# Attention of the first block: the values of one unit ahead of the transposes of the next on TensorE

## The chip, the cores and the metric

The kernel runs on one core of a Trainium2 chip. The core has five engines with a queue of instructions each: TensorE (PE) for matrix products, VectorE (DVE), ScalarE (ACT), GpSimd (POOL) and SyncE (SP), which here issues the DMAs. Each takes its instructions strictly in the order of the program, and waits on semaphores for the others. The metric is the device time of one execution in microseconds.

## The reference

Two transformer blocks of depth 2 each run one after the other on 256 tokens of width 1024. In the first, each layer mixes three kinds of heads, and the attention kinds among them are these:

```python
        s_c = jnp.einsum('bqghd,bngd->bghqn', qb, kc)
        p_c = _masked_softmax(s_c, cmp_end[None, :] <= t[:, None])
        o_c = jnp.einsum('bghqn,bngd->bqghd', p_c, vc)
...
        o_s = jnp.einsum('bghqkl,bgqkld->bqghd', p_s, v_sel)
...
        o_w = jnp.einsum('bghqk,bkgd->bqghd', p_w, vwb)
...
        return gb[:, :, 0, :, :, None] * o_c + gb[:, :, 1, :, :, None] * o_s + gb[:, :, 2, :, :, None] * o_w
```

and, for the third kind of head,

```python
        s = jnp.einsum('bqhd,bkhd->bhqk', qb, kh) + cq[..., None] - c[:, :, None, :]
        p = _masked_softmax(s, kpos[None, :] <= t[:, None])
        return jnp.einsum('bhqk,bkhd->bqhd', p, vh)
```

The second block needs a modulation vector, silu(c) @ w_ada (1024 x 9216 a layer), that depends on nothing in the first.

## The kernel before

The first reference block runs as two layers, l = 0 and 1; below, "block 0" and "block 1" are these two passes through the same code, in which the attention stands once. Their attention lies at 174 to 268 us and 656 to 750 us of the span.

The attention is cut into 22 units (`units_block1`): for each half of the 128-row query tiles (tt = 0, then 1) a "cmp" unit for the compressed keys of all heads, then "slc" and "win" units in turn, four of each, for two heads each, then two "fox" units. In the first half a unit has 128 keys, in the second 256. A unit passes through these steps, each with a semaphore:

- TensorE, `unit_scores` (L986, L997, L1003; L994 and L1002 for fox): scores of the unit into a bank, att_s.
- VectorE, `unit_max`: row maximum (L1072, L1074), att_m.
- ScalarE, `unit_exp` (L1125): exponential and row sum, att_e.
- VectorE, `unit_norm` (L1095 to L1103): the rows scaled by gate over sum, att_p.
- TensorE, `unit_turn` (L1015; L1012 for cmp): the probabilities transposed into bank 6, two or four 128x128 transposes. It waits for att_p of this unit and att_c of the one before; att_t.
- ScalarE, `unit_copy` (L1137; L1132 for cmp): bank 6 to SBUF, att_c.
- TensorE, `unit_values` (L1034; a slc unit has first L1028, the compressed part): probabilities times values into bank 7. It waits for att_c of this unit, and at a unit that opens an output for the output before, att_o; att_v. A cmp unit has none.
- ScalarE, `unit_out` (L1144): bank 7 out, once a win or fox unit is done, att_o.

The loops are software-pipelined by turns n = 0 to 23. On TensorE a turn is: scores of unit n+1, a part of the modulation (`ada_pe`), transposes of unit n-1, values of unit n-2. On VectorE: maximum of unit n, `ada_dve`, norm of unit n-1. On ScalarE: exponential of unit n, copy of n-1, output of n-2, `ada_act`.

The modulation is filled in between: in every turn `ada_pe` takes two 512 KB chunks of w_ada from a ring of four slots (L856, 32-column tiles, 8 rows in the trace) and, in turns 0 and 1 and all odd turns after, folds a finished row first (L844). A fold waits for the ScalarE copy of the row in the turn before (`ada_act`, L866), and VectorE takes the fold's result (L872) in the same turn, ahead of its norm. A slot freed by L856 lets SyncE ask for the chunk four further on. Behind the attention comes the output product (L774 on), whose weights use the same ring.

The order is written out by hand; no scheduler moves it. The loop in question is `attention_pe`, from L1040.

Of the kernel before, what the change touches and what calls it, by code (L numbers as in the profile page):

```python
# [502 lines left out]
def kernel_program(nc, streams, consts, params, x_cm, ctx_cm, out_cm, blocks=(1, 2)):  # L503
    with ExitStack() as stack:
# [320 lines left out]
        def ada_bank(l, q):  # L825
            return bank[1 + 2 * ((ADA_QUADS * l + q) % 2)]

        def ada_chunk(l, i):
            a, own, b = PLAN["in_a", l].chunk, PLAN["ada", l].chunk, PLAN["wo", l].chunk
            chunk = a + 2 * i + 1 if i < 7 else own + i - 7 if i < 7 + ADA_ALONE else b + 2 * (i - 7 - ADA_ALONE) + 1  # L830
            return chunk % SLOTS, chunk // SLOTS

        def ada_started(t):
            return range(ADA_UPTO[t - 1] if t else 0, ADA_UPTO[t])

        def ada_done(t):

            return [q for q in range(ADA_QUADS) if t >= 0 and 4 * q + 3 in ada_started(t)]

        def ada_pe(pe, l, t):  # L840
            for q in ada_done(t - 2):
                pe.wait_ge(s.ada_row, ADA_QUADS * l + q + 1)
                for j in range(4):
                    mm = pe.matmul(ada_bank(l, q)[:, 2 * j:2 * j + 2], ada_row[:, j * P:(j + 1) * P], fold,  # L844
                                   start=True, stop=True)
                mm.then_inc(s.ada_t, 1)
            for m in ada_started(t):
                q, c = m // 4, m % 4
                slot, turn = ada_chunk(l, m)
                if c == 0 and ADA_QUADS * l + q >= 2:  # L850
                    pe.wait_ge(s.ada_out, ADA_QUADS * l + q - 1)
                pe.wait_ge(landed[slot], (turn + 1) * 16)
                for i in range(2):
                    k = 2 * c + i
                    rows = slice(k % COL_GROUPS * COL_GROUP, (k % COL_GROUPS + 1) * COL_GROUP)
                    mm = pe.matmul(ada_bank(l, q)[rows, :], cs[:, k, :], ring[:, slot, i * 4 * P:(i + 1) * 4 * P],  # L856
                                   start=(k < COL_GROUPS), stop=(k >= COL_GROUPS))
                mm.then_inc(used[slot], 1)
# [120 lines left out]
        def unit_scores(pe, x):  # L979
            if x.u >= 2:  # L980
                pe.wait_ge(s.att_e, x.u - 1)
            q = slice(x.tt * P, (x.tt + 1) * P)
            if x.kind == "cmp":
                for h in range(QH):
                    rows = slice(h % 2 * DH, h % 2 * DH + DH)
                    mm = pe.matmul(half_scores(x, h % 2)[:, h // 2 * N_CMP:(h // 2 + 1) * N_CMP], qr[rows, h // 2, q],  # L986
                                   kcb[rows, h // 4 * N_CMP:(h // 4 + 1) * N_CMP], start=True, stop=True)
                mm.then_inc(s.att_s, 1)
                return
            for hh in range(2):  # L990
                rows = slice(hh * DH, hh * DH + DH)
                dst = half_scores(x, hh)[:, 0:x.keys]
                if x.kind == "fox":
                    pe.matmul(dst, qkn[rows, 6 + x.j, q], qkn[rows, 8 + x.j, 0:x.keys], start=True, stop=False)  # L994
                else:
                    key = kd[rows, x.g, 0 if x.kind == "slc" else 1, 0:x.keys]
                    pe.matmul(dst, qr[rows, 2 * x.g + x.j, q], key, start=True, stop=False)  # L997
            for hh in range(2):
                dst = half_scores(x, hh)[:, 0:x.keys]
                if x.kind == "fox":  # L1000
                    for st in range(x.kt):
                        pe.matmul(dst, fa[:, st, 2 * x.j + hh, q], gtk[:, st, 0:x.keys], start=False, stop=False)  # L1002
                mm = pe.matmul(dst[:, x.keys - P:x.keys], ident, causal, start=False, stop=True)  # L1003
            mm.then_inc(s.att_s, 1)

        def unit_turn(pe, x):

            pe.wait_ge(s.att_p, x.u + 1)
            if x.u >= 1:
                pe.wait_ge(s.att_c, x.u)  # L1010
            if x.kind == "cmp":
                mm = pe.transpose(bank[6][0:heads_n, 0:P], pr[:, x.u % 2, 0:heads_n], ident)  # L1012
            else:
                for c in range(2 * x.kt):
                    mm = pe.transpose(bank[6][:, c * P:(c + 1) * P], pr[:, x.u % 2, c * P:(c + 1) * P], ident)  # L1015
            mm.then_inc(s.att_t, 1)
# [3 lines left out]
        def unit_values(pe, x):  # L1020
            if x.kind == "cmp":
                return
            pe.wait_ge(s.att_c, x.u + 1)
            if x.first and x.o >= 1:
                pe.wait_ge(s.att_o, x.o)
            if x.kind == "slc":
                h = 4 * x.g + 2 * x.j
                pe.matmul(bank[7][:, 0:P], own_b[0:heads_n, h * DH:(h + 2) * DH], c_pt[0:heads_n, x.tt, :],  # L1028
                          start=True, stop=False, skip_group_check=True)
            for k in range(x.kt):  # L1030
                for hh in range(2):
                    head = 2 * x.j + hh if x.kind == "fox" else x.g
                    c0 = VCOL[x.kind] + head * DH
                    mm = pe.matmul(bank[7][hh * DH:(hh + 1) * DH, 0:P], vtok[:, k, c0:c0 + DH],  # L1034
                                   pt[:, x.v % 2, (hh * x.kt + k) * P:(hh * x.kt + k + 1) * P],
                                   start=(x.kind == "fox" and k == 0), stop=(x.last and k == x.kt - 1),
                                   skip_group_check=True)
            mm.then_inc(s.att_v, 1)

        def attention_pe(pe, l, units):  # L1040
            unit_scores(pe, units[0])
            for n in range(len(units) + 2):
                if n + 1 < len(units):
                    unit_scores(pe, units[n + 1])
                ada_pe(pe, l, TICK_ATT + n)
                if 1 <= n <= len(units):
                    unit_turn(pe, units[n - 1])
                if n >= 2:
                    unit_values(pe, units[n - 2])

        def unit_max(dve, x):

# [353 lines left out]
        def block1_pe(pe, l):  # L1406
# [87 lines left out]
            pe.wait_ge(s.vc_done, l + 1)  # L1494
            pe.wait_ge(s.fa, l + 1)
            attention_pe(pe, l, units_block1(l))

            lin = PLAN["wo", l]
# [1094 lines left out]
```

## Time and profile before

| | us |
|---|---|
| three timed executions | 3120.65, 3120.95, 3123.78 |
| their median | 3120.95 |
| the profiled execution | 3125.64 |
| its span in the trace | 3123.9 |
| TensorE busy in it | 2961.4 (95%) |
| VectorE busy | 1519.0 (49%) |
| ScalarE busy | 1129.8 (36%) |

The profile is of one execution, not among the three. "Busy" of TensorE has modelled ends, so that durations of neighbours overlap in the timeline; the starts are what was recorded. An fp32 matmul shows as two records, one of fp32r and a transpose as one. A group in the timeline merges like instructions that follow each other, and a wait inside a group shows only as a longer group.

### The profile page before, as it was taken

What the parts mean: (1) busy time and instruction counts of PE and PEld (TensorE: products, weight loads), DVE (VectorE), ACT (ScalarE), POOL (GpSimd) and SP (SyncE); (2) the same over time, 40 slices, a digit from 0 to 9 for tenths busy, and PEclk for the clock granted to TensorE, in tenths of its full rate; (3) what the DMA queues carried; (4) which work ended last, traced back from release to release, by engine and by line L of the source; (5) the groups of instructions that cost most, each with busy time, mean ns of one, the idle gap of its engine ahead of it and who ended that gap; (6) DMA issues with size and microseconds to landing.
All of it is one profiled execution on the core that took longest, in us unless ns stands there. A gap on an engine that the chain in (4) does not pass through costs nothing.

```text
span 3123.9 us, 46087 instructions
## 1 busy us (share of the span) xinstructions
PE 2961.4 (95%) x17140; PEld 2426.9 (78%) x17140; DVE 1519.0 (49%) x2621; ACT 1129.8 (36%) x1727; POOL 45.3 (1%) x36
## 2 busy tenths in 40 slices
PE   6998998989999999999999999999999998999998
PEld 6756998846898888877466678888788887688998
DVE  5344655434656333349433464333433336645664
ACT  4333544333544222133355332222322223385443
POOL 0100000000000000002000000000000000000000
PEclk9999999999999999999999999999999998999999
DMA  4576454476554222321122122223222222234454
GB/s 172 186 264 223 164 179 155 155 275 232 185 175 141 95 94 92 100 84 58 61 74 65 63 85 96 99 92 96 88 94 101 91 99 93 74 116 137 164 181 137
DMA packets 119881, 400.91 MB, mean 128 GB/s; under 512 B 13008, under 2 KB 22608, under 8 KB 119504
## 3 DMA queue, kind: packets, MB, share of 16 engines
q1 hardware_dynamic: 116816, 393.27, 37.5%
q10 hardware_dynamic: 2944, 6.01, 0.5%
q8 instruction: 78, 1.28, 0.2%
q14 instruction: 43, 0.35, 0.0%
HBM read 398.18 MB, written 1.05 MB: 128 GB/s over the span
## 4 chain that ended last, share of the span: by engine, by line
PE 84%; DVE 8%; ACT 3%; DMA 2%; DVEq 2%; issue 1%; ACTq 0%; SPq 0%
PE bank L774 22%; PE bank L781 21%; PE bank L784 21%; PE bank L2130 4%; DVE hid L2383 2%; PE bank L856 2%; DVE w_lo L733 2%; PE bank L1429 2%; DMA ring<-weights 2%; ACT w_hi L705 1%; PE bank L1900 1%; PE bank L1880 1%; DVEq L2389 1%; PE bank L2216 1%; PE bank L844 1%
## 5 line engine op out<-in xcount | busy, mean ns | idle before, releaser
L733 DVE TENSOR_TENSOR w_lo<-ring,w_hi 128x1024 fp32r<-128x1024 f32 (+1 forms) x538 | 650.1, 1209 | 1042.0 <-ACT w_hi L705 1038.3
L705 ACT ACTIVATE w_hi<-ring 128x1024 fp32r<-128x1024 f32 (+1 forms) x538 | 562.9, 1046 | 1380.1 <-PE bank L774 1262.7
L781 PE MATMUL bank<-hn_hi,w_hi 128*128 128x256 f32 (+1 forms) x2816 | 887.5, 335 | 0.0
L784 PE MATMUL bank<-hn_lo,w_hi 128*128 128x256 f32 (+1 forms) x2816 | 886.9, 334 | 0.0
L774 PE MATMUL bank<-hn_hi,w_lo 128*128 128x256 f32 (+1 forms) x2816 | 560.2, 342 | 35.0 <-DVE w_lo L733 23.9
L781 PEld LDWEIGHTS bank<-hn_hi,w_hi 128*128 128x128 f32 x2816 | 538.7, 191 | 52.2
L784 PEld LDWEIGHTS bank<-hn_lo,w_hi 128*128 128x128 f32 x2816 | 538.5, 191 | 52.1
L774 PEld LDWEIGHTS bank<-hn_hi,w_lo 128*128 128x128 f32 x2816 | 444.5, 191 | 117.7 <-issue 63.1
L781 PE MATMUL bank<-hid_hi,w_hi 128*128 128x512 f32 (+1 forms) x704 | 248.8, 363 | 0.0
L784 PE MATMUL bank<-hid_lo_a,w_hi 128*128 128x512 f32 (+1 forms) x640 | 226.2, 363 | 0.0
L774 PE MATMUL bank<-hid_hi,w_lo 128*128 128x512 f32 (+1 forms) x704 | 157.5, 364 | 7.9 <-DVE work L2066 4.8
L781 PEld LDWEIGHTS bank<-hid_hi,w_hi 128*128 128x128 f32 x704 | 132.9, 189 | 20.6
L774 PEld LDWEIGHTS bank<-hid_hi,w_lo 128*128 128x128 f32 x704 | 121.5, 188 | 31.1 <-issue 6.2
L784 PEld LDWEIGHTS bank<-hid_lo_a,w_hi 128*128 128x128 f32 x640 | 120.8, 189 | 18.7
L781 PE MATMUL bank<-up_hi,w_hi 128*128 128x256 f32 x512 | 125.6, 283 | 0.0
L784 PE MATMUL bank<-up_lo,w_hi 128*128 128x256 f32 x512 | 125.6, 283 | 0.0
L2130 PE MATMUL bank<-hid,ring 128*128 128x512 f32 (+1 forms) x352 | 124.3, 494 | 1.3 <-ACT hid L1944 1.3
L2383 DVE SCALAR_TENSOR_TENSOR hid<-work,par,hid 128x512 f32<-128x512 f32 (+1 forms) x180 | 117.4, 706 | 5.0 <-issue 0.5
L856 PE MATMUL bank<-ring,conds 128*32 128x512 f32 x576 | 103.8, 636 | 1.7 <-DMA ring<-weights 1.2
L784 PEld LDWEIGHTS bank<-up_lo,w_hi 128*128 128x128 f32 x512 | 98.3, 192 | 0.0
L781 PEld LDWEIGHTS bank<-up_hi,w_hi 128*128 128x128 f32 x512 | 98.3, 192 | 0.0
L2130 PEld LDWEIGHTS bank<-hid,ring 128*128 128x128 f32 x352 | 63.8, 189 | 42.7 <-issue 38.8
(302 smaller groups left out, 3006.0 us busy)
## 6 DMA issues: line engine op xcount, KB each, us to landing
ring<-weights SPq DMA_DIRECT2D x692, 512.0 KB, 3.3
ring<-weights SPq DMA_DIRECT2D x32, 384.0 KB, 3.0
ring<-weights SPq DMA_DIRECT2D x32, 256.0 KB, 2.6
ring<-weights SPq DMA_DIRECT2D x32, 192.0 KB, 2.3
con<-consts ACTq DMA_DIRECT2D x1, 2063.0 KB, 14.5
ring<-weights SPq DMA_DIRECT2D x16, 128.0 KB, 2.0
con<-consts ACTq DMA_DIRECT2D x1, 1088.0 KB, 5.0
res<-x_cm ACTq DMA_DIRECT2D x1, 1024.0 KB, 10.7
```

The source lines that it names most:

```text
L705: act.activation(w_hi[:, even, 0:w], ring[:, slot, 0:w], ACT.Copy).then_inc(s.w_hi, 1)
L733: eng.tensor_tensor(w_lo[:, even, 0:w], ring[:, slot, 0:w], w_hi[:, even, 0:w].bitcast(F32), ALU.subtract).then_inc(s.w_lo, 1)
L774: mm = pe.matmul(dst, w_lo[:, number % 2, k * P:(k + 1) * P], x_hi(k), start=(start and k == order[0]), stop=False)
L781: pe.matmul(dst, high, x_hi(k), start=False, stop=False)
L784: mm = pe.matmul(dst, high, x_lo(k), start=False, stop=(stop and k == order[-1]))
L844: mm = pe.matmul(ada_bank(l, q)[:, 2 * j:2 * j + 2], ada_row[:, j * P:(j + 1) * P], fold, start=True, stop=True)
L856: mm = pe.matmul(ada_bank(l, q)[rows, :], cs[:, k, :], ring[:, slot, i * 4 * P:(i + 1) * 4 * P], start=(k < COL_GROUPS), stop=(k >= COL_GR ...
L1429: mm = pe.matmul(bank[2 * parity(lin, g)][:, q], sq[:, k, q], ring[:, slot_of(lin, g, 0), k * P:(k + 1) * P], start=(k == 0), stop=(k == K ...
L1880: mm = pe.matmul(scores(x)[:, j * x.keys:(j + 1) * x.keys], q2[0:QK, x.h + j, x.tt * P:(x.tt + 1) * P], k2[0:QK, x.h + j, x.key0:x.key0 + ...
L1900: mm = pe.matmul(bank[7][rows, 0:P], v2[:, x.key0 // P + k, h * DH:(h + 1) * DH], pt[:, x.u % 2, (j * kt + k) * P:(j * kt + k + 1) * P], s ...
L2130: mm = pe.matmul(bank[2 * parity(lin, g)][:, 0:w], ring[:, slot_of(lin, g, 0), k * P:(k + 1) * P], src[:, k, 0:w], start=(k == 0), stop=(k ...
L2383: last = dve.scalar_tensor_tensor(out=dst, in0=src, scalar=taps[:, m, k:k + 1], in1=dst, op0=ALU.mult, op1=ALU.add)
```

## The change

In each turn of `attention_pe`, the values of unit n-2 are issued ahead of the transposes of unit n-1 instead of behind them. The instructions, their operands and their semaphores are the same.

```diff
                 ada_pe(pe, l, TICK_ATT + n)
+                if n >= 2:
+                    unit_values(pe, units[n - 2])
                 if 1 <= n <= len(units):
                     unit_turn(pe, units[n - 1])
-                if n >= 2:
-                    unit_values(pe, units[n - 2])
```

TensorE's order in turns 3 and 4, in the middle of the first half (L844 fold, L856 chunk, L1015 transposes, L1028 and L1034 values, L997 and L1003 scores; - is before, + is now):

```order
 L844 MATMUL bank<-con_64,work 128x2 x4
 L856 MATMUL bank<-ring,conds 32x512 x4
-L1015 MATMUL bank<-con_64,work 128x128 x2
 L1028 MATMUL bank<-work 128x128
 L1034 MATMUL bank<-work 64x128 x2
+L1015 MATMUL bank<-con_64,work 128x128 x2
 L997 MATMUL bank<-hid 128x128 x2
 L1003 MATMUL bank<-con_65,con_64 128x128 x2
 L856 MATMUL bank<-ring,conds 32x512 x4
+L1034 MATMUL bank<-work 64x128 x2
 L1015 MATMUL bank<-con_64,work 128x128 x2
-L1034 MATMUL bank<-work 64x128 x2
```

The transposes of the turn moved from right behind the chunk to right ahead of the next scores, the values the other way.

TensorE's order in turn 20, the last but three, where no scores are left to follow:

```order
 L856 MATMUL bank<-ring,conds 32x512 x4
-L1015 MATMUL bank<-con_64,work 128x128 x4
 L1028 MATMUL bank<-work 128x128
 L1034 MATMUL bank<-work 64x128 x4
+L1015 MATMUL bank<-con_64,work 128x128 x4
```

In turn 20 the transposes now stand directly in front of the fold (L844) of turn 21. In turns 21 and 22 the pair L1015, L1034 is swapped in the same way. The last turn has values alone and is unchanged. On VectorE, ScalarE, GpSimd and SyncE no instruction moved.

## Rows read from the trace of the kernel before

**Rows 1.** Page, part 1: busy time and share of the span, instructions.

```profile
PE 2961.4 (95%) x17140; PEld 2426.9 (78%) x17140; DVE 1519.0 (49%) x2621; ACT 1129.8 (36%) x1727; POOL 45.3 (1%) x36
```

**Rows 2.** Block 0's attention: busy PE, PEld, DVE, ACT, POOL; granted clock, DMA share, GB/s.

```profile
174.00:268.00 94.00, 89.75 (x712) 53.40 (x710) 37.40 (x170) 37.13 (x128) 0.00 (x0) 1.00 0.78 274
```

**Rows 3.** TensorE's timeline, turns 4, 5: start, length, what, [idle <- releaser].

```profile
190.50 1.06 PE L856 MATMUL bank<-ring,conds 128*32 128x512 f32 x8
191.50 0.44 PE L1015 MATMUL bank<-con,work 128*128 128x128 f32 x2
191.87 0.44 PE L1034 MATMUL bank<-work 128*64 128x128 f32 x4
192.24 0.49 PE L997 MATMUL bank<-hid 64*128 64x128 f32 x4
...
193.21 1.02 PE L844 MATMUL bank<-con,work 128*128 128x2 f32 x8
194.16 1.06 PE L856 MATMUL bank<-ring,conds 128*32 128x512 f32 x8
195.35 0.44 PE L1015 MATMUL bank<-con,work 128*128 128x128 f32 x2
195.63 0.39 PE L1028 MATMUL bank<-work 120*128 120x128 f32 x2
```

**Rows 4.** ScalarE's timeline in turn 4.

```profile
192.53 0.59 ACT L866 ACTIVATE work<-bank 128x512 f32<-128x512 f32 x1
```

**Rows 5.** VectorE's timeline in turn 5.

```profile
194.26 0.17 DVE L872 TENSOR_TENSOR mods<-bank,par 128x8 f32<-128x8 f32 x1 [2.92 <-PE bank L844]
```

**Rows 6.** TensorE's timeline, turns 14, 15.

```profile
228.26 0.66 PE L1015 MATMUL bank<-con,work 128*128 128x128 f32 x4
228.75 0.39 PE L1028 MATMUL bank<-work 120*128 120x128 f32 x2
229.07 0.66 PE L1034 MATMUL bank<-work 128*64 128x128 f32 x8
229.66 0.70 PE L997 MATMUL bank<-hid 64*128 64x256 f32 x4
...
230.84 0.95 PE L844 MATMUL bank<-con,work 128*128 128x2 f32 x8
231.72 1.06 PE L856 MATMUL bank<-ring,conds 128*32 128x512 f32 x8
233.05 0.66 PE L1015 MATMUL bank<-con,work 128*128 128x128 f32 x4 [0.26 <-DVE work L1103]
```

**Rows 7.** ScalarE's timeline in turn 14.

```profile
229.44 0.59 ACT L866 ACTIVATE work<-bank 128x512 f32<-128x512 f32 x1
```

**Rows 8.** TensorE's timeline, turns 20 to 23 and the output product.

```profile
256.78 0.66 PE L1015 MATMUL bank<-con,work 128*128 128x128 f32 x4
...
258.61 1.05 PE L844 MATMUL bank<-con,work 128*128 128x2 f32 x8 [0.36 <-ACT work L866]
...
264.97 1.05 PE L844 MATMUL bank<-con,work 128*128 128x2 f32 x8 [0.86 <-ACT work L866]
265.95 1.47 PE L856 MATMUL bank<-ring,conds 128*32 128x512 f32 x8
...
271.61 1.58 PE L774 MATMUL bank<-hn_hi,w_lo 128*128 128x256 f32 x8 [3.60 <-issue]
```

**Rows 9.** ScalarE's timeline in turn 22.

```profile
264.32 0.59 ACT L866 ACTIVATE work<-bank 128x512 f32<-128x512 f32 x1
```

**Rows 10.** TensorE's timeline, turn 23 of block 1.

```profile
746.46 1.83 PE L856 MATMUL bank<-ring,conds 128*32 128x512 f32 x8
```

**Rows 11.** Busy time by stretch, end of block 1's attention.

```profile
744.00:748.00 4.00, 3.14 (x25) 1.49 (x24) 1.30 (x2) 2.30 (x4) 0.00 (x0) 0.83 0.98 376
```

**Rows 12.** TensorE's timeline, turns before block 1's attention.

```profile
650.29 4.76 PE L856 MATMUL bank<-ring,conds 128*32 128x512 f32 x16
```

## Prediction

> **What bounds the kernel now.** I read the page first: TensorE is busy 95% of the span [rows 1], so the question is always what keeps it from starting the next instruction. Then the busy time of the stretch that the change touches, the attention of block 0: TensorE 89.75 of 94 us at full granted clock, the weight stream at 0.78 of the DMA engines, ScalarE and VectorE both under 40% [rows 2]. Then the timeline of TensorE, turn by turn, with ScalarE and VectorE beside it [rows 3 to 9]. What the reader is to see there: a turn of TensorE is scores S, in odd turns a fold F (L844), a vector chunk A (L856), the transposes T (L1015), the values V (L1028, L1034). It is full but for four kinds of gaps. I use the starts of instructions, since the ends are modelled.
>
> There are 24 turns (n = 0 to 23) for 22 units in each block; units 0 and 11 are "cmp" and have no values. The eight "slc" units have L1028 in front of their values. All is worked out for block 0 and doubled, since block 1 runs the same list.
>
> **The change part by part.** Nothing is added or removed; within a turn T and V trade places. T(n-1) waits for VectorE's norm (att_p), V(n-2) only for a copy that ScalarE finished a turn ago. Four terms follow.
>
> *1. The wait for the norm is covered (gain).* In a plain turn A to T is 191.50 - 190.50 = 1.00 us. In a fold turn of the first half it is 195.35 - 194.16 = 1.19, because VectorE first has to take the fold's result (L872 at 194.26 [rows 5]) and T starts 1.09 after that: 0.20 lost [rows 3]. In the second half it is 233.05 - 231.72 = 1.33: 0.33 lost [rows 6]. With V ahead (0.59 or more in the second half, 229.66 - 229.07; at least 0.37 in the first) the wait is over before T's turn comes. There are four such turns in the first half (3, 5, 7, 9) and three in the second with values to put in front (15, 17, 19); turns 1 and 13 have none and keep theirs. Gain 4 x 0.20 + 3 x 0.33 = 1.8 us a block, 3.6 in all. What is late next in these turns is nothing: the next fold is two turns away.
>
> *2. One more change of array shape in each slc turn (loss).* Two transposes take 195.63 - 195.35 = 0.28 when L1028 follows, which has their 128x128 shape, and 191.87 - 191.50 = 0.37 when L1034 (128x64) follows [rows 3]. Afterwards the 64-row scores always follow T, so every one of the 8 slc turns pays 0.09 more: 0.7 a block, 1.4 in all. The Trainium skill (TensorEngine Tiling (Array Packing), Tiling Modes) says that changing the tiling mode, not just the tile, drains TensorE; the trace agrees with 0.09 us here. Were every change of shape free, the sum would be 1.4 us lower. The new joints A to V and V to T occur nowhere in this trace. The nearest rows are joints of unlike shapes that cost 0.09 over like ones; I take them as costly as the joints they replace, and bound each plain turn by 0.09 less and 0.09 more. With some 18 values in a block whose joints count, that is 1.6 us a block, 3.3 in all, on either side.
>
> *3. ScalarE's path to the next fold (loss).* After T, ScalarE does copy, output and ada (L866), and the fold of the next turn waits for L866. Today V runs on TensorE meanwhile. In turn 4, T starts at 191.50, L866 ends at 192.53 + 0.59 = 193.12, and a fold can start 0.06 after such an end (264.32 + 0.59 = 264.91 against 264.97 [rows 8, 9]), at 193.18; it started at 193.21 [rows 3, 4]. There is no slack at all. From T on, ScalarE needs 1.68 us; TensorE will have only T and S, 0.37 + (193.21 - 192.24) = 1.34. So TensorE waits 0.34 in turns 4 and 6. In turn 10 the scores are those of the second half, 230.84 - 229.66 = 1.18, so the wait is 1.68 - 1.55 = 0.13. In turns 14 and 16 ScalarE needs 229.44 + 0.59 + 0.06 - 228.26 = 1.83 [rows 7], TensorE has 0.59 + 1.18 = 1.77: 0.06 each. Where fox scores come in between (8 and 18) the longer scores hide it. A fold that has waited takes 0.95 (194.16 - 193.21) and one that has not 0.88 (231.72 - 230.84) [rows 3, 6]: 0.07 more in four turns. Together 0.68 + 0.13 + 0.12 + 0.28 = 1.2 a block, 2.4 in all.
>
> *4. The end of the attention (loss).* At n = 20 and n = 22 there are no scores left behind T. The folds of turns 21 and 23 already wait for L866, 0.36 and 0.86 us [rows 8]. With V in front of T the same path of ScalarE starts later by the whole of V: 229.66 - 228.75 = 0.91 in turn 20, 0.59 in turn 22, and 0.06 for a bank that V(20) now awaits. That is 1.56. Part is swallowed: the last A takes 1.47 against a usual 1.06, 0.4 of it a wait for its weights (block 1: 1.83, so 0.8) [rows 8, 10]. But those weights are asked for when turn 21 frees their buffer, so they too come about 0.9 later, and only the rest is swallowed. I take 1.05 a block, 2.1 in all, with 0.5 and 1.56 a block as ends. Then the last values and the first weights of the output product (L774 at 271.61) follow as before, shifted.
>
> The other queues (SP, GpSimd) keep their order; SP's requests shift with the A's.
>
> Sum: -3.6 + 1.4 + 2.4 + 2.1 = +2.3 us. Against the profiled execution (span 3123.9, 3125.64 in all) this gives 3127.9; that execution is 4.7 above the median of the runs, 3120.95, so the forecast on the median's scale is 3120.95 + 2.3 = **3123.2**, a change of 0.07%. Changes under 0.2% (6.2 us) count as none, which is about what a measurement of this kernel can tell. With the joints at either bound (3.3) and the tail's ends (1.1 less, 1.0 more) it runs from 3118.8 to 3127.5.
>
> **Rivals.**
>
> *A. The waits are filled and ScalarE's path costs nothing.* For it: 0.34 us is a small gap, and the output (L1144) no longer has to wait for V. Against it: L866 and the fold are 0.03 apart today. It gives -3.6 + 1.4 = -2.2, 3118.7. With free joints as well 3115.5.
>
> *B. The weight stream sets the pace.* For it: 0.78 of the DMA engines [rows 2], four chunks ahead only, and A's that wait, such as the last of either block [rows 8, 10]. Then TensorE's gaps are merely traded for gaps before a chunk, and the change does not do what it says: 3121. Against it: most A's take exactly 1.06.
>
> *C. The clock falls earlier in the tail (slower than before).* In block 1 the mean granted clock is 0.83 in 744 to 748 us, so it falls from the 2.4 to the 1.2 GHz level there, TensorE being busy 3.14 of these 4 us [rows 11]; block 0's attention keeps 1.00 to its end [rows 2]. Term 4 adds a gap of 0.9 at turn 21 and one of 0.6 at turn 23 to both. If the clock is at the 1.2 GHz level from the fold of turn 21 on, chunks cost 4.76/16 = 0.30 us a record, as ahead of block 1's attention [rows 12] instead of 0.125 (1.00 for 8), so three A's of 8 records cost 4.2 more, and two transposes, two values and two folds that double some 3.2 more: 7.4 a block. One block so: 3130.6; both: 3138. It decides once the fold of turn 21, not that of 23, is followed by L856 at 0.30 a record. The Trainium skill (TensorE: Matmul & The Clock Gate, Part 1) holds that TensorE is throttled by default and that activity releases it. By that rule more gaps speak for C; the trace agrees in block 1, where the lower level comes after a wait, and not in block 0, which has the same instructions and waits and holds its level.
>
> **How the numbers follow.** The forecast (3118.8 to 3127.5) 0.55; A 0.12; B 0.20; C 0.06 (one block or both); and 0.07 for something I have not seen, half on either side. Faster by over 0.2% needs 3114.7 or less, which only A with free joints and the unseen reach: 0.04. Slower by over 0.2% needs over 3127.2: C, the upper edge of the forecast and the unseen, 0.07. Within: 0.89. The range takes in A and B whole and leaves out C: 3118 to 3127.5 (the two bounds seldom meet, so little is left out above).
>
> **What would show it.** In the changed profile: (1) in fold turns of the second half T follows V with no idle from VectorE, and only turn 13 keeps its 0.3; (2) T to scores is 0.37 in every turn of the first half; (3) TensorE waits for L866 before the fold in turns 5 and 7, about 0.3 each; (4) the waits of the last two folds rise from 0.36 and 0.86 to about 1.2 and 1.5; (5) the first A after turn 0 and the last T lie nearly as far apart as before, and what the attention loses it loses from turn 20 on. If the waits of (3) are missing, A is right; if the chunk waits change instead, B; if a whole A takes 2.4 in the tail, C. I am wrong altogether if V right behind A costs other than T there did by more than 0.1 us.

## The result: slower by 0.19%, lost for the most part at the end of the attention

On 22 runs each, the changed kernel takes 3130.76 us (3122.88 to 3137.15), the kernel before 3124.99 us (3118.57 to 3131.14). The ratio is 1.0019, 95% interval 1.0011 to 1.0026, which is +5.8 us (3.4 to 8.1). I forecast +2.3. The forecast of 3123.2 is missed by 7.6 us: 4.0 because the median of the three runs I had of the kernel before stood that far under its median of 22, and 3.5 because of the change. Chips and runs scatter by 6 us to either side, so only ratios, and stretches of the traces, are compared below.

The page of the changed kernel, part 1:

```profile
PE 2969.2 (95%) x17140; PEld 2427.5 (78%) x17140; DVE 1519.0 (49%) x2621; ACT 1127.7 (36%) x1727; POOL 45.2 (1%) x36
```

TensorE holds 95% as in [rows 1], with the same instructions. The profiled span is 6.9 us longer than before, but that is the balance of larger differences: the two attentions and their ends took 11.2 us more, and the stretches that the change does not touch 4.3 us less (1.7 less ahead of block 0's attention, 2.1 more between the two, 4.7 less behind the second). So the spans of two executions don't measure the change; stretches do. Two kinds of turns show what it does.

TensorE's timeline in turns 4 and 5 of block 0 (start, length, engine, line, what; the answer to [rows 3]):

```profile
190.67 0.44 PE L1034 MATMUL bank<-work 128*64 128x128 f32 x4
191.04 0.44 PE L1015 MATMUL bank<-con,work 128*128 128x128 f32 x2
191.41 0.49 PE L997 MATMUL bank<-hid 64*128 64x128 f32 x4
191.83 0.71 PE L1003 MATMUL bank<-con,con 128*128 128x128 f32 x4
192.60 1.05 PE L844 MATMUL bank<-con,work 128*128 128x2 f32 x8
193.59 1.06 PE L856 MATMUL bank<-ring,conds 128*32 128x512 f32 x8
194.59 0.49 PE L1028 MATMUL bank<-work 120*128 120x128 f32 x2
195.00 0.44 PE L1034 MATMUL bank<-work 128*64 128x128 f32 x4
```

Below, S, F, A, T and V are the prediction's names: scores, fold (L844), chunk (L856), transposes (L1015) and values (L1028, L1034). V to T and T to scores take 0.37 each (191.04 - 190.67, 191.41 - 191.04). The fold comes 0.77 after L1003, where it came 0.55 after it before (L1003 at 192.66, between the rows of [rows 3]): 0.22 of waiting for L866, as the step said, if smaller. In the fold turn L1028 follows A after 1.00 as T did in a plain turn; the 0.19 of waiting of [rows 3, 5] is gone. L1028 to L1034 is 195.00 - 194.59 = 0.41.

The same in turns 14 and 15 (answer to [rows 6]):

```profile
227.53 0.49 PE L1028 MATMUL bank<-work 120*128 120x128 f32 x2
227.94 0.66 PE L1034 MATMUL bank<-work 128*64 128x128 f32 x8
...
230.36 1.05 PE L844 MATMUL bank<-con,work 128*128 128x2 f32 x8
231.35 1.06 PE L856 MATMUL bank<-ring,conds 128*32 128x512 f32 x8
232.34 0.66 PE L1034 MATMUL bank<-work 128*64 128x128 f32 x8
232.93 0.66 PE L1015 MATMUL bank<-con,work 128*128 128x128 f32 x4
```

Turn 15 has lost its 0.33: 232.34 - 231.35 = 0.99. Here too L1028 to L1034 takes 0.41; [rows 6] have 229.07 - 228.75 = 0.32. This joint, with A in front of L1028 instead of T, is the 0.09 that I had not priced.

TensorE's timeline in turns 21 to 23 of block 1 and the output product (answer to [rows 8]):

```profile
750.01 1.05 PE L844 MATMUL bank<-con,work 128*128 128x2 f32 x8 [1.17 <-ACT work L866]
751.00 1.24 PE L856 MATMUL bank<-ring,conds 128*32 128x512 f32 x8
752.17 1.12 PE L1034 MATMUL bank<-work 128*64 128x128 f32 x8
753.22 1.11 PE L1015 MATMUL bank<-con,work 128*128 128x128 f32 x4
754.27 1.49 PE L856 MATMUL bank<-ring,conds 128*32 128x512 f32 x8
...
758.27 1.05 PE L844 MATMUL bank<-con,work 128*128 128x2 f32 x8 [1.34 <-ACT work L866]
...
764.20 1.19 PE L774 MATMUL bank<-hn_hi,w_lo 128*128 128x256 f32 x8 [3.29 <-issue]
```

and the busy time there (columns as in [rows 2]):

```profile
750.00:753.00 3.00, 2.98 (x24) 1.84 (x24) 1.54 (x7) 0.87 (x4) 0.00 (x0) 0.79 0.44 179
753.00:756.00 3.00, 3.00 (x22) 1.24 (x20) 0.00 (x0) 0.77 (x2) 0.00 (x0) 0.64 0.89 302
```

The fold of turn 21 waits 1.17 where [rows 8] have 0.36, that of turn 23 1.34 instead of 0.86. Behind the first of them the granted clock is 0.79 and 0.64 of full, a mean over the 2.4 and the 1.2 GHz level, which in these two stretches of 3 us makes (0.21 + 0.36) x 3 x 2 = 3.4 us at the lower one. V and T of turn 21, of 8 and 4 records, take 1.05 each (753.22 - 752.17, 754.27 - 753.22) instead of 0.59. Block 0 shows the same from 260.2 to 263.6 us.

Three lengths sum it up, all between starts on TensorE (S0, S11: scores of units 0 and 11; A20: chunk of turn 20; P: first L774 of the output product):

| us | block 0 before | block 0 changed | block 1 before | block 1 changed |
|---|---|---|---|---|
| S0 to S11 | 37.70 | 38.18 | 36.23 | 43.24 |
| S11 to A20 | 44.00 | 44.18 | 43.23 | 42.89 |
| A20 to P (tail) | 15.83 | 18.02 | 16.35 | 18.02 |

The 7 us in S0 to S11 of block 1 stands out; the first experiment deals with it.

### The profile page after: what moved, and what is told of

Same layout as the page of the kernel before. It is cut to its first block, busy times and chain, and to the rows that moved or that the text cites. A ratio compares the mean times of both kernels' runs of the same rounds, so it can differ in the third digit from the quotient of the medians.

```text
span 3130.8 us, 46087 instructions
## 1 busy us (share of the span) xinstructions
PE 2969.2 (95%) x17140; PEld 2427.5 (78%) x17140; DVE 1519.0 (49%) x2621; ACT 1127.7 (36%) x1727; POOL 45.2 (1%) x36
## 3 DMA queue, kind: packets, MB, share of 16 engines
HBM read 398.18 MB, written 1.05 MB: 128 GB/s over the span
## 4 chain that ended last, share of the span: by engine, by line
PE 84%; DVE 8%; ACT 3%; DMA 2%; DVEq 1%; issue 1%; ACTq 0%; SPq 0%
PE bank L774 22%; PE bank L784 21%; PE bank L781 21%; PE bank L2130 4%; PE bank L856 3%; DVE hid L2383 2%; DMA ring<-weights 2%; DVE w_lo L733 2%; PE bank L1429 2%; ACT w_hi L705 1%; PE bank L1900 1%; PE bank L1880 1%; DVEq L2389 1%; DVE hn_lo L941 1%; PE bank L2216 1%
## 5 line engine op out<-in xcount | busy, mean ns | idle before, releaser
L774 PE MATMUL bank<-hn_hi,w_lo 128*128 128x256 f32 (+1 forms) x2816 | 558.5, 341 | 34.5 <-DVE w_lo L733 23.7
L774 PEld LDWEIGHTS bank<-hn_hi,w_lo 128*128 128x128 f32 x2816 | 443.3, 190 | 117.0 <-issue 62.5
L774 PE MATMUL bank<-hid_hi,w_lo 128*128 128x512 f32 (+1 forms) x704 | 157.5, 364 | 7.9 <-DVE work L2066 4.8
L774 PEld LDWEIGHTS bank<-hid_hi,w_lo 128*128 128x128 f32 x704 | 121.5, 188 | 31.1 <-issue 6.2
L856 PE MATMUL bank<-ring,conds 128*32 128x512 f32 x576 | 106.4, 660 | 2.9 <-DMA ring<-weights 2.3
```

What stands on the lines that cost most here:

```text
L774: mm = pe.matmul(dst, w_lo[:, number % 2, k * P:(k + 1) * P], x_hi(k), start=(start and k == order[0]), stop=False)
```

## Experiments

Theory T: the time is lost in the tail, by longer waits for L866 and a clock that falls behind the first. Rival J: it is lost at the new joints all over the attention. Rival U: it is lost at the start of block 1's attention, in and ahead of its first turns. "New order" is values first. Each ratio is the time over that of the kernel before, with its 95% interval.

### again: the changed kernel a second time

> The changed kernel once more, for a second trace. Measured so far, from the first chunk of turn 20 to the first L774 of the output product: 15.83 and 16.35 us before (block 0, block 1), 18.02 and 18.02 after; from the scores of unit 11 to turn 20: 44.00 and 43.23 before, 44.18 and 42.89 after; and 7 us more in and ahead of block 1's first turns. Theory T (the loss sits in the tail: longer waits for L866, and a granted clock that falls behind the first of them): both tails 17.8 to 18.3 again, with L1034 x8 and L1015 x4 of turn 21 at about 1.05 us instead of 0.59, slower by 3 to 6 us in time. Theory U (what was lost ahead of block 1's attention belongs to the change): the scores of unit 0 to unit 11 in block 1 take 43 us again instead of 36. By T that stretch returns to about 36 to 38 in this trace, being a matter of the single execution.

No edit. Ratio 1.0029 (1.0017 to 1.0042), +9.0 us (5.3 to 13.1); with the first result it agrees only where the two intervals overlap, 5.3 to 8.1. Tails 16.64 and 19.72 us, not the 17.8 to 18.3 I expected: they scatter more. Block 0's, on TensorE:

```profile
258.80 1.05 PE L844 MATMUL bank<-con,work 128*128 128x2 f32 x8 [1.18 <-ACT work L866]
...
260.78 0.66 PE L1034 MATMUL bank<-work 128*64 128x128 f32 x8
261.37 0.66 PE L1015 MATMUL bank<-con,work 128*128 128x128 f32 x4
...
271.61 1.79 PE L774 MATMUL bank<-hn_hi,w_lo 128*128 128x256 f32 x7 [3.29 <-issue]
```

The same wait of 1.18 stands before the fold, and yet V and T keep 0.59: here the clock did not fall, and the tail is 1.38 us shorter than 18.02. In block 1 it fell twice, at 746.1 behind the wait of 1.18 and at 753.0 behind that of 1.34, and the tail is longer. So the fall behind that first wait is frequent, not certain.

S0 to S11 in block 1 took 39.93 us: not the 43 that U asked for, and not the 36 to 38 of T either. The granted clock at its start, in before, the changed kernel, this one and tail_filled (below), in that order:

```profile
660.00:665.00 5.00, 4.07 (x34) 2.06 (x33) 2.19 (x12) 1.14 (x5) 0.00 (x0) 1.00 0.62 243
```

```profile
660.00:665.00 5.00, 5.00 (x34) 4.73 (x32) 0.90 (x4) 0.30 (x1) 0.00 (x0) 0.50 0.63 247
```

```profile
660.00:665.00 5.00, 4.74 (x30) 2.94 (x34) 0.74 (x4) 1.40 (x5) 0.00 (x0) 0.66 0.57 194
```

```profile
660.00:665.00 5.00, 4.93 (x25) 2.96 (x23) 1.56 (x8) 0.00 (x0) 0.00 (x0) 0.50 0.61 215
```

1.00, 0.50, 0.66, 0.50, in turns that the change does not touch (the first swap is in turn 3). TensorE had waited for weights just before, 0.79, 1.99, 1.74 and 0.77 us:

```profile
655.84 1.05 PE L856 MATMUL bank<-ring,conds 128*32 128x512 f32 x4 [0.79 <-DMA ring<-weights]
```

```profile
658.87 1.25 PE L856 MATMUL bank<-ring,conds 128*32 128x512 f32 x4 [1.99 <-DMA ring<-weights]
```

```profile
656.42 1.05 PE L856 MATMUL bank<-ring,conds 128*32 128x512 f32 x4 [1.74 <-DMA ring<-weights]
```

```profile
654.22 1.05 PE L856 MATMUL bank<-ring,conds 128*32 128x512 f32 x4 [0.77 <-DMA ring<-weights]
```

The length of that wait does not tell which execution falls: 0.77 has a fall behind it and 0.79 none. The turns 0 to 2 of block 1, whose TensorE instructions are the same in all kernels here, from S0 to the chunk of turn 3:

| trace | order | us | granted clock |
|---|---|---|---|
| before | old | 12.6 | 1.00 |
| late_only | new in turns 15, 17, 19 | 12.6 | 1.00 |
| tail_old | new in the body | 12.6 | 1.00 |
| tail_only | new in the tail | 12.6 | 1.00 |
| plain_only | new in even turns | 17.2 | 0.70 |
| changed kernel | new | 19.1 | 0.57 |
| again | new | 15.8 | 0.78 |
| tail_filled | new, idle matmuls | 16.3 | 0.69 |
| row_first, row_warm, row_mixed_warm | new (mixed: but for slc turns), row first | 14.0 | 0.88 |
| row_first_old | old, row first | 12.5 | 1.00 |

All five traces with the new order in every turn have the fall, by 1.4 to 6.5 us, and so do row_mixed_warm and plain_only, which have it in a part of the turns; the five others have none. So U is not refuted: the traces rather point to the change having a part in it, through what it does to block 0. If such a fall came with every execution of the changed kernel, some 4 us more (6.5, 3.1 and 3.7 in the first three) would have to be added to the 5.5 that the rest of the traces account for (below): 9.5, above the interval of the first result (3.4 to 8.1) and inside that of this one (5.3 to 13.1). How much of it belongs to the change stays open.

### tail_old: the change in turns 0 to 19 only

```diff
+                ahead = n < 20
+                if n >= 2 and ahead:
+                    unit_values(pe, units[n - 2])
                 if 1 <= n <= len(units):
                     unit_turn(pe, units[n - 1])
-                if n >= 2:
+                if n >= 2 and not ahead:
                     unit_values(pe, units[n - 2])
```

> The change in turns 0 to 19 only; turns 20 to 22 in the old order (transposes first). T: tails back to 15.8 to 16.4 us, waits for L866 0.36 and 0.86 again, body as after; time within 1.5 us of before (ratio 0.9995 to 1.0005). Rival J (the joints in the body, V right behind A, cost the time): still slower by 3 us or more (ratio 1.001 and up).

Ratio 0.9996 (0.9985 to 1.0008). Tails 16.54 and 15.11, the latter without any wait for weights or loss of clock. Its fold of turn 21:

```profile
742.01 1.05 PE L844 MATMUL bank<-con,work 128*128 128x2 f32 x8 [0.36 <-ACT work L866]
```

S0 to S11 and S11 to A20 in block 1, both without a wait for weights, 36.73 and 42.89. In the old order S0 to S11 without such waits is 36.22, and S11 to A20 is 43.23 less 0.40 that turn 10 of it waited for its chunk, 42.83. The body thus costs 0.5 + 0.1 us a block. J asked for a ratio of 1.001 and up, outside of the interval: it falls as the main cause.

### tail_only: the change in turns 20 to 22 only

The same edit with `ahead = n >= 20`.

> The change in turns 20 to 22 only, body as before. T: tails 17.8 to 18.3 us in both blocks, time 3 to 5 us over before (ratio 1.001 to 1.0016). J: tails cost the 1.05 us a block that I forecast, time within 2.2 us of before.

Ratio 1.0008 (0.9994 to 1.0022), a point just under what T said (1.001 to 1.0016) and an interval that excludes neither T nor J nor no change. The trace decides for the tail: 18.05 and 18.02, with bodies of 38.07, 43.71, 36.22 and 43.05, those of the old order. In block 1:

```profile
742.14 1.05 PE L844 MATMUL bank<-con,work 128*128 128x2 f32 x8 [1.18 <-ACT work L866]
...
744.66 1.12 PE L1034 MATMUL bank<-work 128*64 128x128 f32 x8
745.71 1.12 PE L1015 MATMUL bank<-con,work 128*128 128x128 f32 x4
```

The tail alone makes the tail's loss. By time the two halves of the change do not make the whole: -1.2 us (-4.7 to 2.5) and +2.5 us (-1.9 to 6.9) against the +9.0 of again. The intervals are wide enough to allow it, barely; U, if it needs both halves, would also do it.

### tail_filled: work in the waits before the last folds

```diff
+                for _ in range({20: 4, 22: 5}.get(n, 0)):
+                    if n == 20 and _ == 0:
+                        pe.wait_ge(s.att_e, units[20].u + 1)
+                    pe.matmul(bank[4][:, 0:P], ident, ident, start=True, stop=True)
```

The `wait_ge` holds the first of them until ScalarE's exponential of unit 20 is done.

> The changed kernel with idle matmuls (identity by identity, into bank 4, which nobody reads any more) behind the transposes of turn 20 (4) and of turn 22 (5), where TensorE waits 1.18 and 1.34 us for L866. If the clock falls because of these waits (T, part clock), L1034 x8 and L1015 x4 of turn 21 take 0.59 each at granted clock 1.00, and the tails come down by 1.2 to 1.6 us each, to about 16.5. If only the longer path of ScalarE counts and the clock is indifferent to it, the tails stay at 18.0.

Ratio 1.0002 (0.9990 to 1.0014). Tails 17.21 and 16.52. In block 1:

```profile
741.75 1.06 PE L1053 MATMUL bank<-con 128*128 128x128 f32 x8
743.09 1.05 PE L844 MATMUL bank<-con,work 128*128 128x2 f32 x8 [0.28 <-ACT work L866]
...
745.07 0.66 PE L1034 MATMUL bank<-work 128*64 128x128 f32 x8
745.65 0.66 PE L1015 MATMUL bank<-con,work 128*128 128x128 f32 x4
...
748.34 1.28 PE L1053 MATMUL bank<-con 128*128 128x128 f32 x10
749.85 1.05 PE L844 MATMUL bank<-con,work 128*128 128x2 f32 x8 [0.23 <-ACT work L866]
```

```profile
743.00:746.00 3.00, 2.91 (x27) 1.89 (x28) 1.55 (x7) 0.95 (x5) 0.00 (x0) 1.00 0.47 191
746.00:749.00 3.00, 3.00 (x29) 1.82 (x28) 0.00 (x0) 1.23 (x3) 0.00 (x0) 1.00 0.85 322
```

A20 to the fold is 743.09 - 739.25 = 3.84, as in the changed kernel (750.01 - 746.18 = 3.83), so ScalarE's path is unaltered; only TensorE is not idle in it. V and T of turn 21 take 0.59 in both blocks at granted clock 1.00. The tails come down by 1.2 on the mean of the two; in block 1 to what the path alone asks for, in block 0 the last chunk takes 0.7 more. That in two blocks of two the clock held, and fell in five of six unfilled ones (counting tail_only), supports the cause without making it a law. By the ratios the time fell by 8 us against again, more than these 2.4 us: the interval lies wholly under that of again (1.0017 to 1.0042), although this trace has the fall at the start of block 1. What made the rest is not shown.

### late_only: the gain without the price

`ahead = n in (15, 17, 19)`.

> The change in turns 15, 17 and 19 only, where a wait of 0.33 us for the norm stands and the unit has no L1028. T: the three waits vanish, nothing else changes, so the scores of unit 11 to turn 20 take 1.0 us less than in the old order (about 42.5 against 43.0 to 44.0), tails as before (15.1 to 16.5), about 2 us faster in all: ratio 0.9994, within the interval of no change. Rival (V in front of T always costs something at the new joints): no gain in that stretch.

Ratio 0.9994 (0.9982 to 1.0007). S11 to A20 in block 1 is 41.85 us, 0.98 under 42.83: three waits of 0.33, gone. Block 0's 44.29 holds chunks that waited 0.7 and 1.1 us for their weights. Tails 17.01 (2.37 us in the last chunk, with the clock at its lower level from 264.1 on) and 15.11. For these turns of block 1 term 1 of the prediction was right to a hundredth; it is below what the time can show.

### plain_only: the price without the gain

`ahead = n < 20 and n % 2 == 0`.

> The change in the even turns 2 to 18 only, the turns that have no wait for the norm, so the price without the gain. T: TensorE waits for L866 before the fold 0.24 us in turns 5 and 7 and 0.03 to 0.06 in 11, 15, 17; the slc turns 14, 16, 18 cost 0.19 each (one more change of shape, and L1028 to L1034 0.41 instead of 0.32); the waits of 0.20 and 0.33 for the norm stay. So from the scores of unit 11 to turn 20 0.7 us more than before, tails as before; 2 to 3 us slower in all (ratio 1.0007). If the path of ScalarE is not what delays the folds, no waits ahead of L844 appear.

Ratio 1.0009 (0.9999 to 1.0019). The fold after turn 4:

```profile
191.17 0.71 PE L1003 MATMUL bank<-con,con 128*128 128x128 f32 x4
191.95 1.05 PE L844 MATMUL bank<-con,work 128*128 128x2 f32 x8
```

0.78 instead of 0.55, and the same 0.78 before the fold of turn 7, in both blocks; 0.57 in 11, 0.61 in 15 and 17. S11 to A20 in block 1 is 43.90, no chunk waiting: 1.07 above 42.83, where I had 0.7, since a fold that has waited here takes 0.98 instead of 0.88. Term 3's mechanism is shown. Its size: 0.23 instead of 0.34, as the output on ScalarE (L1144) no longer waits for the values: it starts 0.28 behind the start of the copy L1137 (191.79 - 191.51, changed kernel, turn 4) and not 0.38 (192.35 - 191.97, before).

### row_first: the row for the fold ahead of the copy

```diff
+                ada_act(act, l, TICK_ATT + n)
                 if 1 <= n <= len(units):
                     unit_copy(act, units[n - 1])
                 if n >= 2:
                     unit_out(act, units[n - 2])
-                ada_act(act, l, TICK_ATT + n)
```

> The changed kernel, and on ScalarE in every turn the row for the fold (L866) ahead of the copy of the transposes instead of behind copy and output. L866 needs only the chunks of the turn before, so it ends long before the fold. If the path T, copy, output, L866, fold makes the waits (T), those of 1.18 and 1.34 us before the last two folds vanish, and with them the cold stretch behind them: tails 13.8 to 15.5 us instead of 16.6 to 19.7; time 2 to 4 us under before (ratio 0.9987 to 0.9995). The last chunk may then wait for its weights instead (up to 1.5 us), which gives part back. If the folds were held by something else, the tails stay over 16.6.

Ratio 0.9977 (0.9967 to 0.9988) with the new order on TensorE, a larger gain than the 0.9987 to 0.9995 that I expected. L1003 to L844 is 0.55 wherever it was 0.55 to 0.78, and the last folds of block 1 wait for nothing:

```profile
741.77 0.66 PE L1015 MATMUL bank<-con,work 128*128 128x128 f32 x4
742.27 0.95 PE L844 MATMUL bank<-con,work 128*128 128x2 f32 x8
...
747.04 0.66 PE L1015 MATMUL bank<-con,work 128*128 128x128 f32 x4
747.53 0.95 PE L844 MATMUL bank<-con,work 128*128 128x2 f32 x8
```

Tails 16.07 and 14.26. Counted turn by turn in block 1, with the waits for chunks left out, the block takes 2.4 us less than before: 4.8 in all, in the lower part of the interval of 3.8 to 10.3. In block 0 the gain was partly returned to the weights:

```profile
260.00 1.05 PE L856 MATMUL bank<-ring,conds 128*32 128x512 f32 x4 [1.50 <-DMA ring<-weights]
```

The path T, copy, output, L866, fold is what the last folds waited for, since taking L866 out of it removes the waits.

### row_first_old: the same with the old order

> The kernel before (transposes first), with L866 ahead of the copy on ScalarE. T: the waits of 0.36 and 0.86 us before the last two folds vanish; tails 13.8 to 15.5 us; in the body the folds of turns 5 and 7 start no later than now. Time 1.5 to 3 us under before (ratio 0.9990 to 0.9996); the order of T and V then matters by at most 2 us against row_first, the price of the one being the gain of the other.

The kernel before with the edit of row_first. Ratio 0.9990 (0.9979 to 1.0000). No fold waits; tails 15.91 and 14.32, S11 to A20 keeps its waits of 0.26 for the norm. The traces see next to no difference from row_first in the tail; that the two ratios differ by 0.0013 is not significant by their intervals. So the tail's loss was not in the swap as such but in what L866 stood behind.

### row_warm: and the wait before the output product filled

The edit of row_first, and the idle matmuls as in tail_filled with `{23: 11}`.

> As row_first, and behind the last values of each attention eleven idle matmuls (identity by identity into bank 4), 2.9 us of work in the 3.3 us that TensorE waits for the first weights of the output product. Theory T (the clock falls for want of work there, and the product starts at the lower level): the first L774 x8 takes 1.2 us instead of 2.0 and the L781 and L784 behind it start 0.12 apart from the first on, 1.5 to 3 us less for both blocks: ratio 0.997. If the clock is indifferent to this filling, L774 x8 stays at 1.4 to 2.0 and the time at row_first's, 0.9977.

Ratio 0.9980 (0.9967 to 0.9992): not better than row_first. The product did start at the higher level, in block 0 and 1 alike, but ran ahead of its weights:

```profile
266.94 1.19 PE L774 MATMUL bank<-hn_hi,w_lo 128*128 128x256 f32 x8 [0.64 <-issue]
...
277.65 1.19 PE L774 MATMUL bank<-hn_hi,w_lo 128*128 128x256 f32 x8 [1.78 <-DVE w_lo L733]
```

```profile
275.19 1.06 ACT L705 ACTIVATE w_hi<-ring 128x1024 fp32r<-128x1024 f32 x1 [6.25 <-DMA ring<-weights]
```

The first L774 x8 takes 1.19 us instead of the 2.04 of row_first's block 0, and the third waits 1.78 us for a split that waited for its chunk. By the ninth group of L774 nothing is left of the gain in block 0: it starts 53.26 us after the first, as in before (53.32). In block 1 it was kept, 50.52 against 53.48 in row_first and 53.59 in before, and row_mixed_warm has 50.52 there too. These 3 us are what I had expected of both blocks at most, and less than the time can show.

### row_mixed_warm: slc turns left in the old order

As row_warm with `ahead = n >= 2 and units[n - 2].kind != "slc"`.

> As row_warm, but values ahead of transposes only where the unit is not slc; slc turns keep the old order. T: in turns 14, 16, 18 and 20 the 0.19 us of the extra change of shape and of L1028 to L1034 come back, in the first half the 0.20 of the wait for the norm returns in their place: 0.7 us less than row_warm in a block between the scores of unit 11 and turn 20, 1.5 us or 0.05% in all, which the time can't show but the trace can (L1028 to L1034 0.32 again, transposes 0.49 instead of 0.59).

Ratio 0.9970 (0.9957 to 0.9983), the fastest of all, with a median of 3114.04 against 3125.38 for the kernel before. S11 to A20 in block 1 is 41.95 us (row_warm's 44.21 holds a chunk that waited 1.1, so that the expected 0.7 can't be read from the two), and in turn 20 L1028 to L1034 takes 0.31 again. The interval overlaps row_warm's and row_first's: over the kernels before and after it is shown to be faster, over row_first it is not.

## Why the prediction was wrong, step by step

**Term 1 (the norm's wait is covered)** was right: 0.33 gone in turns 15, 17 and 19, 0.2 in the first half's fold turns, and turns 1 and 13 keep theirs. 1.8 us a block. Turn 17 of block 0 I had not looked at: it waits 0.62 for the norm there, of which V covers all but 0.1, so that block gains 0.26 more.

**Term 2 (one more change of shape in slc turns)** was right in what it counted, 0.09 for T, and lacked as much again: L1028 to L1034 takes 0.41 behind A, 0.32 behind T. I had bounded that joint by 0.09 and taken zero. A to V and V to T cost what the old joints cost. 0.18 in each of the seven slc turns of the body, 1.3 us a block; turn 20 has no scores behind T (T to fold takes 0.49 in row_first) and its 0.09 for the joint stands in the tail.

**Term 3 (L866 and the folds in the body)** happened in each turn that I named; waits of 0.23, 0.23, 0.02, 0.06, 0.06 against 0.34, 0.34, 0.13, 0.06, 0.06. The size was too large because I let the output on ScalarE wait for V as before, though rival A had named it. With the 0.04 to 0.10 that these folds take longer, 1.0 a block instead of 1.2.

Together the body comes to +0.5 a block by these terms, and 0.6 by tail_old's trace; I had forecast 0.1.

**Term 4 (the tail) is the step that failed: it put the fall of the clock at nothing.** It has three parts. The path: the waits grew as said, to 1.18 and 1.34, and the position of V alone is worth 1.4 us, turn by turn +1.00, -0.10, +0.50 and 0 (tail_filled's block 1 at 16.52 against tail_old's 15.11, both at full clock and without a wait for weights); I had 1.56. What is swallowed: I had 0.5, read from the last chunk. In the eight tails of the old order (before, tail_old, late_only, plain_only) the mean is 15.92, so 0.8 over 15.11 is lost to late chunks and to the clock, and in the new order the last chunk takes 1.0 in four of six tails; the swallowing took place. But of block 1's chunk of 1.83 us I read 0.8 as a wait for weights, and it is the clock, at its lower level from 746.6 to 752 at least:

```profile
745.00:748.00 3.00, 2.53 (x16) 1.12 (x16) 1.30 (x2) 1.36 (x2) 0.00 (x0) 0.77 0.95 358
748.00:752.00 4.00, 1.34 (x12) 0.72 (x8) 1.39 (x2) 1.85 (x3) 0.00 (x0) 0.50 0.67 236
```

The third part I left to rival C. Behind the wait of 1.18 the clock fell in five of the six tails in the new order, each time for some 3.4 us; in turns 21 and 22 of the old order, behind 0.36, it fell in none of eight. A tail with one such fall takes 18.02, 1.5 more than its path. The mean tail in the new order is 18.08: 2.16 a block more than in the old one, where I said 1.05.

The sum by the traces is 2 x (0.57 + 2.16) = +5.5 us, against +5.8 (3.4 to 8.1) in time. That they agree so closely is in part luck, since again gave +9.0 and the traces hold the open 3 to 6.5 us at the start of block 1 besides.

**Rivals.** A (ScalarE's path costs nothing) is refuted by plain_only; where row_first makes it true, the time is 0.9977 of before. B (the weights set the pace) holds in single turns only. C was right in place and mechanism and wrong in length: I let the lower level last from the fold of turn 21 to the end, three chunks long, and priced it at 7.4 us a block; it cost 1.5, often. It was also priced wrongly by the piece: a whole chunk at the lower level takes 1.87 us (259.32 to 261.19 in tail_only), not the 2.4 I took from 4.76/16, and the 3.2 for the other items counts one of the two folds, 4 x 0.59 + 2 x 0.88 being 4.1. As a small and likely loss the clock belonged in the sum, and I gave it 0.06. That the measured 3130.76 lies beside C's 3130.6 is chance, as 4.0 of it is the kernel before.

Open: why the clock held in one tail of six behind the same wait of 1.18. The length of a wait does not decide it: behind the 1.34 before the fold of turn 23 it fell in one tail of six, and behind the 0.86 there in the old order in two of eight (each up to the last values). And whether the fall at the start of block 1's attention comes more often with the change is not settled; with the scatter of 6 us between runs it takes many traces.

## What to carry to other kernels

An engine that waits in one turn and is waited for in the next has a price for being late: before moving work in front of what another engine waits for, follow that engine's queue to the next thing TensorE needs, and compare starts for slack; 0.03 us was all there was in turn 4 here. Look at the last turns of a pipelined loop apart from its body, since the work that hides a delay is missing there and the clock may fall on top. Where an item is late only for standing behind an unrelated one in its queue (the row copy behind the transposes' copy), try moving that item first: here the new order with the row moved takes 0.9977 of the kernel before (row_first), and without it 1.0019; the old order with the row moved takes 0.9990 (row_first_old).

## What was not expected of the hardware

- The cost of going from a 128x128 to a 128x64 matmul depends on what ran before the first: L1028 to L1034 starts 0.32 us apart behind transposes of 128x128 and 0.41 behind the 128x32 chunks, in all twelve traces.
- A wait of 1.18 us for L866 was followed in five of six tails by a fall of the granted clock to its lower level for about 3.4 us, starting 0.7 to 2.0 us after the wait had ended, and not during it. The longer wait of 1.34 us two turns later was followed by one in one tail of six. Four idle matmuls in the first wait and five in the second went with a clock of 1.00 in both blocks of the one trace.
- Two executions of the same kernel differ by 3.3 us in one stretch (43.24 and 39.93 from S0 to S11, the changed kernel and again), and turns 0 to 2 of block 1, the same TensorE instructions in all kernels, take 12.5 to 19.1 us at a granted clock of 1.00 to 0.57. The wait for weights just before them, 0.77 us with a fall and 0.79 without, does not sort them.
